# Two transformer blocks in one kernel: modulation products turned by VectorE and folded by one matmul, the first block's last update placed inside the second block, and context products kept in a buffer of their own

## What is computed

```python
def first_block(x, c, ...):                       # 2 layers
    for l in range(2):
        shift, scale, gate = split(silu(c) @ w_mod[l] + b_mod[l], 3)
        h = rms_norm(x, pre_gain) * (1 + scale) + shift
        aq, ak, av, ag, rq, rk, rv, rg, gq, gk, gv, gg, ga = split(h @ w_in[l])
        log_a = log_sigmoid(ga @ gla_gate_w + gla_gate_b) / 16    # ga: 16 columns
        y = concat(attention * silu(ag), retention * silu(rg), gated_linear_attention * silu(gg)) @ w_out[l]
        x = x + gate * rms_norm(y, post_gain)

def second_block(x, c, ctx, c_ctx, ...):          # 2 layers, h_ctx = ctx (256 rows)
    for l in range(2):
        six columns each for x (from c) and for the context (from c_ctx): silu(.) @ w_ada[l] + b_ada[l]
        for rows in (x, h_ctx):                   # the last layer leaves h_ctx as it is
            h = rmsnorm(rows, g_pre_mix) * (1 + sc1) + sh1
            q, k, v, u, g, f = split(h @ w_in[l])
            y = concat(attention, spatial gating, fourier_mix(f)), each normed, @ w_out[l]
            rows = rows + g1 * rmsnorm(y, g_post_mix)
            h = rmsnorm(rows, g_pre_ff) * (1 + sc2) + sh2
            rows = rows + g2 * rmsnorm(square(relu(h @ w_ff1)) @ w_ff2, g_post_ff)
```

## Time and profile before

| | value |
|---|---|
| median of three runs | 4049.59 us (4043.0 to 4055.41) |
| the profiled execution, its own time | 4051.51 us |
| its span in the trace | 4049.7 us |
| mean granted TensorE clock | 0.968 |
| PE busy | 3747.1 us, 93% of the span |
| DVE, ACT, POOL busy | 51%, 43%, 44% |

### The profile page before, as it was taken

How to read it: one execution, slowest core, us unless ns; L and a number is a source line. 1 busy time by engine, 2 the same in 40 slices (tenths; PEclk the granted TensorE clock), 3 DMA queues, 4 the chain that set the end, 5 groups by cost and what they waited for, 6 DMA issues and landing times. The chain is left out here.

```text
span 4049.7 us, 61803 instructions
## 1 busy us (share of the span) xinstructions
PE 3747.1 (93%) x22636; PEld 3023.7 (75%) x22636; DVE 2071.5 (51%) x3220; ACT 1746.5 (43%) x2935; POOL 1775.4 (44%) x1288
## 2 busy tenths in 40 slices
PE   4999999999997799887999899999899899999997
PEld 3777867777775687756888897887687678887886
DVE  5445545545444567656323655226667664235234
ACT  3355355355354544545323454225444563333233
POOL 1443534444442422224545696444322355455444
PEclk8999999999998999988999999999999999999998
DMA  6333433433432321112223453222221122323322
GB/s 249 126 122 120 141 123 116 143 125 120 138 111 95 109 77 52 58 53 84 93 90 97 130 181 110 93 93 89 81 82 58 58 78 94 93 92 95 94 95 102
DMA packets 127207, 421.28 MB, mean 104 GB/s; under 512 B 17408, under 2 KB 19088, under 8 KB 126352
## 3 DMA queue, kind: packets, MB, share of 16 engines
q1 hardware_dynamic: 120080, 407.45, 30.8%
q10 hardware_dynamic: 6912, 10.90, 0.8%
HBM read 397.32 MB, written 6.29 MB: 100 GB/s over the span
## 5 line engine op out<-in xcount | busy, mean ns | idle before, releaser
L1845 POOL TENSOR_TENSOR wlo<-late_raw,whi 128x512 fp32r<-128x512 f32 x456 | 637.6, 1422 | 793.5 <-PE lin L2609 503.7
L1845 POOL TENSOR_TENSOR wlo<-wraw,whi 128x512 fp32r<-128x512 f32 x452 | 633.9, 1427 | 724.3 <-PE lin L2609 501.5
L2600 PE MATMUL lin<-h_hi,whi 128*128 128x512 f32 (+1 forms) x1896 | 715.0, 384 | 49.9 <-ACT y L2147 17.8
L2600 PE MATMUL lin<-h_lo,whi 128*128 128x512 f32 (+1 forms) x1896 | 702.1, 377 | 0.0
L505 POOL TENSOR_TENSOR wlo<-wraw,whi 128x512 fp32r<-128x512 f32 x260 | 362.1, 1413 | 456.3 <-PE lin L1156 295.7
L2600 PE MATMUL lin<-a_hi,whi 128*128 128x512 f32 (+1 forms) x1280 | 474.8, 378 | 16.6 <-ACT tmp L2156 11.2
L2600 PE MATMUL lin<-a_lo,whi 128*128 128x512 f32 (+1 forms) x1280 | 471.7, 375 | 0.0
L2600 PEld LDWEIGHTS lin<-h_hi,whi 128*128 128x128 f32 x1896 | 368.4, 194 | 135.0 <-issue 27.1
L1864 ACT ACTIVATE whi<-late_raw 128x1024 fp32r<-128x1024 f32 x228 | 239.1, 1057 | 530.3 <-PE lin L2600 412.2
L1864 ACT ACTIVATE whi<-wraw 128x1024 fp32r<-128x1024 f32 x226 | 237.3, 1058 | 498.7 <-PE lin L2600 417.5
L2609 PE MATMUL lin<-h_hi,wlo 128*128 128x512 f32 (+1 forms) x1896 | 440.3, 375 | 0.5
(11 more groups left out here) (368 smaller groups left out, 6460.4 us busy)
## 6 DMA issues: line engine op xcount, KB each, us to landing
wraw<-in_w SPq DMA_DIRECT2D x332, 512.0 KB, 3.5
late_raw<-in_w SPq DMA_DIRECT2D x212, 512.0 KB, 3.5
mod_ring<-in_w_ada SPq DMA_DIRECT2D x96, 512.0 KB, 4.5
mod_ring<-in_w_mod SPq DMA_DIRECT2D x32, 512.0 KB, 4.7
turn<-turn SPq DMA_DIRECT2D x144, 64.0 KB, 2.0
first_ring<-in_w_mod SPq DMA_DIRECT2D x16, 512.0 KB, 17.3
wraw<-in_dft_tokens SPq DMA_DIRECT2D x16, 512.0 KB, 3.6
late_raw<-in_dft_tokens SPq DMA_DIRECT2D x16, 512.0 KB, 3.5
```

Source lines behind the costliest of these rows:

```text
L1845: last = nc.gpsimd.tensor_tensor(wlo[:, s, half], raw_chunk[r][:, half], whi[:, s, half].bitcast(F32), ALU.subtract)
L2600: last = nc.tensor.matmul(bank[s][:, 0:p.w], whi[:, s, k * P:(k + 1) * P], h[:, k, 0:p.w], start=(k == 0 and h is parts[0]), stop=False)
```

## The change

The turning of the modulation's rows goes from ACT to DVE, which transposes the bank in blocks of 32 by 32, and one matmul with the matrix `fold` (128 x 128, 48 moving columns) takes the place of four; the bias is then added by four operations on 32 partitions each. The transposes stand behind each `argument` in the startup, and at the end of the steps with s % 4 = 1 in the units. The fold stands in step 3, 7, 11, 14, 18, 23, 27 and 31. `gate_rank` uses 16 matmuls of 32 weight columns. Buffers are shared across the blocks (y, tmp, rstd, mods, cols1, gains2). The last unit's sum, root and update are placed in the second block's first project, with waits on x_done for whoever reads half 1 of x, or the memory of y. Eight of the nine constants are loaded from SP's queue, and `dft_ctx` from ACT's at step 4. Context products go to `y_context`, in the memory of `f`. The first feed forward's squares in layer 0 are taken in the merge of half 1 (steps 4 to 6), summed at step 1 of the context's merge, and the scaling is two tiles per step. In the context's feed forward half 0's updates are one for each hidden chunk 4 to 7, and one after every second output. In the feed forward of half 1, `sum_pre(later)` is one step later.

```diff
+FOLD_AT = [4 * g + (2 if g in (3, 4) else 3) for g in range(8)]
...
+    c["fold"] = (np.arange(P)[:, None] % 32 == np.arange(P)[None, :] % 32).astype(f)
...
+def fold_products(nc, out, fold, turned):
+
+    blocks = turned.rearrange("p (b r) -> p b r", r=32)[:, :, 0:VEC]
+    return nc.tensor.matmul(out.rearrange("p (b v) -> p b v", v=VEC), fold, blocks, start=True, stop=True)
+
...
+def biased(nc, mods, sums, bias, n):
+
+    for q in range(4):
+        part = slice(32 * q, 32 * q + 32)
+        last = nc.vector.tensor_tensor(mods[part], sums[part].rearrange("p (n q v) -> p n q v", q=4, v=VEC)[:, :, q, :],
+                                       bias[part].rearrange("p (n o) -> p n o", o=1).to_broadcast([32, n, VEC]), ALU.add)
...
-            for g in range(groups):
-                act.wait_ge(summed, MOD_GROUP * (g + 1))
-                if g >= 2:
-                    act.wait_ge(turned, g - 1)
-                nc.scalar.activation(row[:, g % 2, :], psR[g % 2][:], ACT.Copy).then_inc(row_ready, 1)
...
-                for c in range(MOD_GROUP):
-                    at = VEC * (g * MOD_GROUP + c)
-                    last = nc.tensor.matmul(psM[:, at:at + VEC], row[:, g % 2, c * P:(c + 1) * P], t["vector_rows"][:],
-                                            start=True, stop=True)
-                last.then_inc(turned, 1)
+                at = 4 * VEC * MOD_GROUP
+                fold_products(nc, psM[:, at * g:at * (g + 1)], t["fold"][:], row[:, g % 2, :]).then_inc(turned, 1)
...
+            def turn_products(g):
+
+                dve.wait_ge(summed, MOD_GROUP * (g + 1))
+                if g >= 2:
+                    dve.wait_ge(turned, g - 1)
+                nc.vector.transpose(row[:, g % 2, :], psR[g % 2][:]).then_inc(row_ready, 1)
...
                     argument(j, cosine)
+                    turn_products(2 * j + 1 - cosine)
...
-        gate_y = sb("gate_y", [P, KB, W])
+        gate_y, rstd = t["y"], t["rstd"]
...
-            def mod_rows(it, s):
...
-                nc.scalar.activation(mod_row[:], bankM[:], ACT.Copy).then_inc(*mod_row_ready.one)
...
-            y_root(UNITS - 1)
...
+            def mod_rows(it, s):
...
+                nc.vector.transpose(mod_row[:], bankM[:]).then_inc(*mod_row_ready.one)
...
+                biased(nc, mods[:, q:q + MOD_GROUP, :], bankM[:, 0:4 * VEC * MOD_GROUP], t["mod_bias"][:, q:q + MOD_GROUP],
+                       MOD_GROUP).then_inc(*mod_out.one)
...
-                if it == 3 and s == 30:
-                    columns2(nc, t, link, 1)
...
-                    if s % 4 == 2:
+                    if s in FOLD_AT:
                         mod_columns(it, s)
...
                     mixers(it, 2 * s + 1)
+                    if s % 4 == 1:
+                        mod_rows(it, s)
...
-            update(UNITS - 1)
...
+                    for n, h in enumerate((h_hi, h_lo)):
+                        last = nc.tensor.matmul(bankE[0:2 * GATE_RANK, :], t["ga_both"][:, KB * l + k, :], h[:, k, :],
+                                                start=(k == n == 0), stop=(k == KB - 1 and n == 1))
...
-                elif s % 4 == 2:
+                elif s in FOLD_AT:
...
-            y_summed(UNITS - 1)
...
+        def product_rows(p):
+            return y_context if p.context else y
...
+        EARLY_SUMS = slots(2), staged[:, 6, :], staged[:, 7, :]
+
+        def ff_squares(l, b, k):
+
+            first_ff = pre_ff(l, FF_ROWS[l][0])
+            if l == 0:
+                return (first_ff, {4: (0, 1, 2), 5: (3, 4, 5), 6: (6, 7)}.get(k, ()) if b == 1 else ())
+            return (first_ff, squares_at(1, k) if b == MERGE_ROWS[l][-1] else ())
+
+        FF_SUM_AT = [1, 5]
+
+        def ff_scales(l, k):
+
+            at = k - FF_SUM_AT[l] - 1
+            per = 2 if l == 0 else 4
+            return range(per * at, min(per * at + per, KB)) if at >= 0 else ()
...
+                if g == RAW2 - 1:
+                    for name, dst in (("ctx", xc[:]), ("mask2", mask_f), ("sinks2", neg_sink[:]), ("dft_dims", dims[:]),
+                                      ("w_sgu", w_s[:]), ("b_sgu", b_s[:]), ("g_sgu", g_s[:]), ("g_mix", g_m[:])):
+                        sp.dma_start(dst, a[name]).then_inc(consts_in.sem, 16)
...
+                elif n.rows.b == 1:
+                    act.wait_ge(*x_done.after(LAST, KB))
...
+                    elif p.in_no == 0:
+                        act.wait_ge(*x_done.after(LAST, 4))
...
+                    if p.in_no == 0 and s == 1:
+                        act.wait_ge(*y_sum.after(LAST, 1))
+                        link(nc.scalar.activation(rstd[:], turnT[1], ACT.Ln, scale=1.0 / D, bias=EPS))
+                        nc.scalar.activation(rstd[:], rstd[:], ACT.Exp, scale=-0.5).then_inc(*y_rstd.one)
...
+                        else:
+                            act.wait_ge(*x_done.after(LAST, KB))
+                            act.dma_start(dft_ctx, a["dft_ctx"]).then_inc(dft_in.sem, 16)
...
-                    if prev:
+                    if prev and not p.context:
                         act.wait_ge(*updated.after(prev.no, k + 1))
-                    nc.scalar.activation(y[:, k, 0:p.w], bank[s][:, 0:p.w], ACT.Copy).then_inc(*lin_free.one)
+                    nc.scalar.activation(product_rows(p)[:, k, 0:p.w], bank[s][:, 0:p.w], ACT.Copy).then_inc(*lin_free.one)
...
+            def update_first(k):
...
+                link(nc.vector.tensor_tensor(y[:, k, :], y[:, k, :], rstd[:], ALU.mult))
+                nc.vector.scalar_tensor_tensor(x[:, k, p.cols], y[:, k, :], t["cols1"][:, DEPTH - 1, C_G + k:C_G + k + 1],
+                                               x[:, k, p.cols], ALU.mult, ALU.add).then_inc(*x_done.one)
...
+                        if p.in_no == 0 and s == 4:
+                            columns2(nc, t, link, DEPTH - 1)
...
                     if j >= 4:
-                        update(prev, 2 * j - 8)
-                        update(prev, 2 * j - 7)
+                        for k in (j - 4,) if p.context else (2 * j - 8, 2 * j - 7):
+                            update(prev, k)
                 dve.sem_inc(wait_seat, 1)
-                outputs(g0, True)
+                if p.context:
+                    for k in range(KB):
+                        output(g0 + FF_CH + k, k % 2, product_rows(p)[:, k, 0:p.w], True)
+                        if k % 2:
+                            update(prev, 4 + k // 2)
+                else:
+                    outputs(g0, True)
...
                         by_blocks(g, 0, p, ready if n.no >= 0 else None, between=between)
+                        if p.in_no == 0:
+                            pe.wait_ge(*y_add.after(LAST, KB - 1))
+                            nc.tensor.matmul(turnT[1], ones[:], POST_SUMS[0][0], start=True, stop=True).then_inc(*y_sum.one)
...
+                    pe.wait_ge(dft_in.sem, 16)
...
-                    if ff and k == 5:
+                    if ff and k == FF_SUM_AT[l]:
                         sum_pre(ff, turnT[0])
...
-                        if k == 5:
+                        if k == 6:
                             pe.wait_ge(*norms["pre"]["rstd"].after(nxt.no, 1))
                             sum_pre(later, turnT[0])
```

More of the change, by code:

```diff
@@ L1205, in gate_rank @@
                 for k in range(KB):
-                    at = slice(k * GATE_RANK, (k + 1) * GATE_RANK)
-                    for n, (w, h) in enumerate(((t["ga_hi"], h_hi), (t["ga_hi"], h_lo), (t["ga_lo"], h_hi))):
-                        last = nc.tensor.matmul(bankE[0:GATE_RANK, :], w[:, l, at], h[:, k, :],
-                                                start=(k == 0 and n == 0), stop=(k == KB - 1 and n == 2))
+                    for n, h in enumerate((h_hi, h_lo)):
+                        last = nc.tensor.matmul(bankE[0:2 * GATE_RANK, :], t["ga_both"][:, KB * l + k, :], h[:, k, :],
+                                                start=(k == n == 0), stop=(k == KB - 1 and n == 1))
                 last.then_inc(*ga_done.one)
@@ L1392, in mod_step @@
                         mod_products(nc, bankM, c * P, cact, mod_ring, c).then_inc(*mod_summed.one)
-                elif s % 4 == 2:
+                elif s in FOLD_AT:
                     pe.wait_ge(*mod_row_ready.after(g, 1))
-                    for c in range(MOD_GROUP):
-                        last = nc.tensor.matmul(bankM[:, VEC * c:VEC * c + VEC], mod_row[:, c * P:(c + 1) * P], t["vector_rows"][:],
-                                                start=True, stop=True)
-                    last.then_inc(*mod_turned.one)
+                    fold_products(nc, bankM[:, 0:4 * VEC * MOD_GROUP], t["fold"][:], mod_row[:]).then_inc(*mod_turned.one)
             def mixers(it, at):
```

149 lines of the change are left out of this document (80 added, 69 removed).

## The result

The changed kernel takes 4017.68 us, the median of four runs (4015.34 to 4019.05), against 4050.2 us before: the ratio is 0.9916, with a 95% interval of 0.9902 to 0.9929. The forecast was 4011.5. The profiled executions stand at 4049.7 and 4013.6 us of span, 36.1 apart, a little more than the medians' 32.5, since the one shown of the changed kernel is the quickest of its four (their spans are 4013.6, 4015.4, 4016.4 and 4017.3).

A forecast was written before the change was run, and what follows sets the result against it. PE, busy 93% of the span, was taken to bound the kernel. Terms 3.5 - 8 - 19.2 - 8.5 - 6.5 + 0.5 = -38.2 gave 4013.3 us for the execution, 4011.5 against the median; range 3990 to 4032.

The forecast's parts named there:

- the likeliest case: Whole kernel: all terms come as forecast, 4011.5 us; chance 0.45.
- bad ends: Whole kernel: all terms at their unfavourable bounds, put at some 4036 us.
- near 1877: Context's merge: the feed forward starts there instead of at 1885.5, by adding DVE's list.
- Startup: Before the first chunk: DVE's wait of 1.4 us and three transposes of 0.69 delay the last argument, +3.5 us.
- Units: First block's units: fewer gate_rank matmuls and cheaper folds, less a late fold in step 14; -2 us each, -8 in all.
- Step 14: Each unit: transpose queued behind DVE's rotation, PE waits 2.45 us plus 1 for half clock, +3.5; such waits only there.
- Border: Between the blocks: small operations, sum, root and updates leave DVE's chain, -19.2 us; bounds -21 and -15.
- eight h_lo (5.4): Border: DVE's eight h_lo operations stay in the remaining chain and take 5.4 us.
- Merge: Context's merge: ACT's copy to y waits for nothing, updates no longer gate PE, feed forward starts earlier; -8.5 us.
- Feed forward: Context's first feed forward: one update per hidden chunk lets outputs begin earlier, -6.5 us; bounds -10 and -3.
- the rival in which PE's waits change their names only: Context's merge and feed forward: DVE binds them as before, the 15 us don't come, 4026.5; chance 0.17.
- The slower rival (late folds throughout): Units: DVE falls behind the folds; gain gone from 8 of 28 late, 4098 us with 16; chance 0.03.

The follow-up runs named there:

- start_act: Changed kernel with only the startup back on ScalarE's copies and four small matmuls a group: first product starts at 72.64 us against 76.38.
- gate_24: Changed kernel with only gate_rank back at 24 matmuls of 16 weight columns a unit: first product to last 1162.79 us, 8.0 more; span 4028.5.
- turn_early: Changed kernel with VectorE's transpose issued ahead of the second half of its step's mixers: span 4006.1 against 4013.6, first product to last 1142.43 against 1154.76.
- copy_waits: Changed kernel with ScalarE's copy in the context's merge waiting again for half 1's update of the same number: 46.52 us against 46.95 there; span 4017.0.
- two_slots: Changed kernel with ScalarE's squares in the context's merge alternating between two banks: 47.04 us against 50.13 to the feed forward; span 4002.9.
- two_a_chunk: Changed kernel with half 0's updates in the context's feed forward back to two per hidden chunk 4 to 7: 1004.1 us against 999.2; span 4021.2.
- fold_30: Changed kernel with a unit's last fold in step 30 instead of 31: first product to border 1167.60 us against 1166.35; span 4018.9.
- act_copies: Changed kernel with the units back on ScalarE's copy and four small matmuls: first product to last 1155.46 us against 1154.76; span 4021.1.
- border_back: Changed kernel with the last unit's sum, root and update back at the end of the first block: span 4033.7, 20.1 more.

## Why the prediction was right, and where not

The forecast of 4011.5 was 6.2 us low, inside its range, and the likeliest case held. Part of that closeness is luck: border and merge brought 7.3 us less than forecast, and 5.0 of it came back in two stretches where losses were forecast (1.0 in the second block up to the merge, 0.5 at the end) and 0.56 and 2.90 us were gained. The working also has two slips. Its bad ends add up to 4039.5 and not to 4036. And the merge's start "near 1877" is given without the list that it is said to come from.

- **Startup**: right, 3.35 for 3.5. The transpose cost what the copy of a bank did, and start_act gives it all back.
- **Units**: right in sum (8.33 for 8) and in mechanism. gate_24 puts it at gate_rank's 8 matmuls. Step 14 was named with its cause, and turn_early shows it. The wait was 2.93; the prediction says 2.45, though its own rows (498.59 to 501.6) give 3.0. The step is 4.15 us longer in three units (10.65 from low product to low product for 6.50) and 2.55 in the first, where I had 3.5; the 1.6 between them is the half clock, which I had at 1. The prediction took it from one row and said that no row shows such a wait free of it. The trace of the kernel before has some, as the 1.10 at 804.03 shows. On the page "TensorE: Matmul & The Clock Gate" of the Trainium skill, activity releases the throttle, and I had read it so that such a wait need not cost any clock. That came true in one unit of four (granted clock 1.00 behind the fold) and not in the three others (0.72 in unit 1). What I missed: some of that loss comes back at the waits behind it, PE waits three times 2.73 for the bias at the next unit's first products, and a fold costs 0.14, not 0.22. Folds also wait 0.81 in step 27 of each unit, so "in step 14, and only there" was too narrow.
- **Border**: the step that failed here is the size of one term, "eight h_lo (5.4)". Its row had no POOL work beside it. With the twelve small operations gone the same eight come 3.4 us sooner behind PE's last product, beside POOL's two operations, and they took 7.20. The 4.6 us of the small operations held 2.1 of the same kind (1.27 and 1.19 where the others took 0.17), so taking them out moved that cost to its neighbours. "GPSIMD Engine Reference" of the Trainium skill has the two engines share SBUF interfaces for two-input operations; the 7.20 beside POOL's 2.93 agrees. The remaining 0.6 is that DVE ended the seam later behind PE (1.65 after the last product's start, 1.04 before). The sum inside the second block cost 0.45, from 1250.40 to the next matmul's 1250.85, not 1.0.
- **Merge**: wrong in mechanism, for its larger part. "The copy waits for nothing" failed: it stands on ACT behind a square that waits for DVE's addition behind the same updates. The step that failed is the wait of 8.41 struck out with the buffer: 13.1 us of waits for ACT's copies became 12.4. 3.73 us came instead of 8.5 (at the feed forward's very first product, which the prediction counts to, it is 6.2: 52.39 became 46.18 us, and 2.5 are lost again two matmuls later, where PE waits 3.24 for a copy). copy_waits shows that the buffer brought none of them, and two_slots wins 3.1 more by one more bank. This is the rival in which PE's waits change their names only, true of the merge and false of the feed forward.
- **Feed forward**: right, 6.28 for 6.5, and two_a_chunk loses 5 to 6 of it.
- **The rest**: 2.90 us less behind the context's outputs, unforecast. It is inside the 5.6 between the thirteen kernels whose code is the same there, so it isn't told from spread. Why the start of the second block falls in the one or the other group is shown only so far as the long update of 1.63 beside POOL goes; that the order of the two comes from the length of the first block is argued, not shown.

The slower rival (late folds throughout) didn't come: but for the four of step 14, the longest wait of a fold is 0.81 us, in step 27, where the working had expected 0.5. Its mechanism is real, as fold_30's 2.76 shows.

## What to carry to other kernels

When a wait is taken off an instruction, look at what stands ahead of it on its own queue, and what that waits for: a scratch buffer with one place ties its writer to the reader's whole list, and a second place was worth more (3.1 us) than the large buffer of its own (nothing). An operation that is moved on a busy in-order engine should go right behind what it needs, not to the end of its step; here that was 12 us of the first block for one line moved. A wait that is taken from one step may only stand in the next: fold_30 lengthens a step by 4.9 us, the seam behind gives it back, and only the time to the border says so. Work that is moved into a stretch with slack makes that stretch depend on who begins first: three edits of the first block alone (turn_early, act_copies, gate_24) lengthened the second by 4.5 to 4.9 us each up to the scores. And a gain is read in the stretch that was edited: the span of two_slots said 10.7, its merge 3.1.

## What was not expected of the hardware

A two-input operation of DVE on 128x512 takes 0.69 to 0.75 us alone and up to 1.78 when it begins while POOL is at work; begun ahead of POOL it took 0.75 in eight traces of twelve. So a chain of them has a length that depends on when it runs: the same eight h_lo took 5.39 and 7.20. One and the same wait of PE may or may not be followed by half clock: 2.93 us before the fold of step 14 (three units of four), 1.97 us behind the border (the kernel before and border_back, not the changed kernel). A transpose of a 128x512 bank from PSUM takes 0.72 us, and a fold's one fp32 matmul of 48 columns 0.14 us of PE's time where its weights are waited for by nobody, against 0.89 for four with three columns each.
